# A decoder layer step on one core: page loads as one run, compress weights awaited round by round, a store moved behind the second pages

## The reference

```python
def _compress(rows, w1, b1, w2, b2, pe):          # rows (n, L, 2, 64), L = 1024 (+4), stride 16, window 32
    sub = rows[:, :n_sub * 16].reshape(n, n_sub, 16, 2, 64)
    first = einsum('nspgd,pdh->nsgh', sub, w1[:16])
    second = einsum('nspgd,pdh->nsgh', sub, w1[16:])
    hid = first[:, :-1] + second[:, 1:] + (einsum('pd,pdh->h', pe, w1) + b1)
    return einsum('ncgh,hd->ncgd', gelu(hid), w2) + b2
```

## Time and profile before

| | |
|---|---|
| median of 3 runs | 1866.27 us (1863.54 to 1869.59) |
| the profiled execution's own time | 1865.92 us |
| its span, first to last instruction | 1863.8 us |
| TensorE busy | 1775.2 us, 95% |
| VectorE busy | 938.5 us, 50% |
| ScalarE busy | 544.7 us, 29% |
| mean granted clock of TensorE | 0.977 |
| DMA packets | 98308, of them under 512 B 40637 |
| moved | 145.60 MB |

### The profile page before, as it was taken

How to read it: one execution, slowest core, us unless ns; L and a number is a source line. 1 busy time by engine, 2 the same in 40 slices (tenths; PEclk the granted TensorE clock), 3 DMA queues, 4 the chain that set the end, 5 groups by cost and what they waited for, 6 DMA issues and landing times. The chain is left out here.

```text
span 1863.8 us, 28616 instructions
## 1 busy us (share of the span) xinstructions
PE 1775.2 (95%) x12010; PEld 1625.7 (87%) x12010; DVE 938.5 (50%) x1876; ACT 544.7 (29%) x1098; POOL 249.8 (13%) x110
## 2 busy tenths in 40 slices
PE   8999989589999899999978999999999999999997
PEld 6889978357767769999848999999999999999996
DVE  6422130467787664341533455545545555554547
ACT  7421000168888622210432221111111111111221
POOL 0111200000000000000000023313313322322320
PEclk9999999779999999999989999999999999999998
DMA  5122657621102241110261111101101101101102
GB/s 197 38 72 58 211 140 198 194 92 58 57 24 72 92 155 60 35 57 29 108 248 46 46 51 69 57 12 68 57 12 68 61 8 68 69 2 67 57 17 94
DMA packets 98308, 145.60 MB, mean 78 GB/s; under 512 B 40637, under 2 KB 73597, under 8 KB 96541
## 3 DMA queue, kind: packets, MB, share of 16 engines
q1 hardware_dynamic: 94094, 140.62, 22.7%
q10 hardware_dynamic: 4088, 3.17, 0.6%
HBM read 132.69 MB, written 14.19 MB: 79 GB/s over the span
## 5 line engine op out<-in xcount | busy, mean ns | idle before, releaser
L1963 PE MATMUL ps<-ff_in_high,ff_weights_low 128*128 128x352 f32 x1032 | 335.0, 325 | 0.0
L1963 PE MATMUL ps<-ff_in_high,ff_weights_high 128*128 128x352 f32 x1032 | 332.6, 322 | 0.0
L1963 PE MATMUL ps<-ff_in_low,ff_weights_high 128*128 128x352 f32 x1032 | 330.5, 320 | 0.0
L1963 PEld LDWEIGHTS ps<-ff_in_high,ff_weights_high 128*128 128x128 f32 x1032 | 194.4, 188 | 0.2
L1963 PEld LDWEIGHTS ps<-ff_in_low,ff_weights_high 128*128 128x128 f32 x1032 | 194.0, 188 | 0.2
L1963 PEld LDWEIGHTS ps<-ff_in_high,ff_weights_low 128*128 128x128 f32 x1032 | 193.7, 188 | 0.0
L2195 DVE TENSOR_TENSOR x<-ps,x 128x352 f32<-128x352 f32 x216 | 113.3, 524 | 134.6 <-PE ps L1981 134.6
L1932 POOL TENSOR_TENSOR ff_weights_low<-ff_weights,ff_weights_high 128x1024 fp32r<-128x1024 f32 x44 | 105.7, 2402 | 418.1 <-ACT ff_weights_high L2077 418.1
L1981 PE MATMUL ps<-ff_act_high,ff_down_high 128*128 128x352 f32 (+1 forms) x496 | 158.4, 319 | 0.2
L1981 PE MATMUL ps<-ff_act_high,ff_down_low 128*128 128x352 f32 (+1 forms) x496 | 156.6, 316 | 0.0
L1981 PE MATMUL ps<-ff_act_low,ff_down_high 128*128 128x352 f32 (+1 forms) x496 | 156.6, 316 | 0.0
(11 more groups left out here) (360 smaller groups left out, 3723.4 us busy)
## 6 DMA issues: line engine op xcount, KB each, us to landing
ff_weights<-in_w_up SPq DMA_DIRECT2D x22, 512.0 KB, 4.0
ff_weights<-in_w_gate SPq DMA_DIRECT2D x22, 512.0 KB, 4.3
ff_down<-in_w_down SPq DMA_DIRECT2D x22, 512.0 KB, 3.5
top<-in_mem_kt SPq DMA_DIRECT2D x8, 1024.0 KB, 10.9
top<-in_mem_v SPq DMA_DIRECT2D x8, 1024.0 KB, 13.5
x<-in_xt SPq DMA_DIRECT2D x3, 1408.0 KB, 10.0
x<-in_pool_cmp SPq DMA_DIRECT2D x32, 128.0 KB, 3.1
big<-in_pool_cmp SPq DMA_DIRECT2D x32, 128.0 KB, 2.8
```

The lines of the kernel that those rows point to most:

```text
L1963: last = nc.tensor.matmul(K.bank[3 * s + x][:, 0:b - a], wt[:, s, ws], h[:, k, a:b], start=k + n == 0, stop=k == KD - 1 and n == 2)
```

## The change

It has five parts. `gather` copies a page as one run of 1 KB a partition, so that in SBUF pages follow one another, each with its keys and values (and heads) inside; TensorE's operands of the compress rounds, of `score` and of the value products are rearranged to match. The gains are loaded behind the first quarter of `w_v`, and ScalarE and VectorE wait for them later; ScalarE makes one copy of `eps` ahead of its first wait. TensorE waits for the values' compress weights ahead of the second round; the bias column is made separately for keys and values, each behind its round, with a second buffer for `terms`, and ScalarE's second GELU waits for the second one. The store of `FM[:, 4:8]` moves from the end of mixer_inputs to compress_phase, behind the windows of the first four sequences.

```diff
...
     regs = K.page_regs = K.page_regs or [sp.alloc_register(f"page{b}") for b in range(NPAGE)]
-    slots = K.slots[half]
-    if name == "cmp":
-        slots = slots.rearrange("p v (g t) -> p v g t", g=HKV)
     with sp.Fori(first, first + count) as n:
...
             of = K.pools[name][bass.ds(page, 1)]
-            of = of.rearrange("a p v g t -> (a p) v g t" if name == "cmp" else "a p v t -> (a p) v t")
-            to = slots[:, :, :, bass.ds(n * (NPAGE * PAGE // 2) + b * (PAGE // 2), PAGE // 2)] if name == "cmp" else \
-                slots[:, :, bass.ds(n * (NPAGE * PAGE) + b * PAGE, PAGE)]
+            of = of.rearrange("a p v g t -> (a p) (v g t)" if name == "cmp" else "a p v t -> (a p) (v t)")
+            to = K.slots[half][:, bass.ds(n * (NPAGE * 2 * PAGE) + b * (2 * PAGE), 2 * PAGE)]
             sp.dma_start(to, of).then_inc(K.slots_came[half], 16)
...
-            sp.dma_start(K.gains[:, :, :], I["gains"]).then_inc(const_came, 16)
             for kk in range(4):
...
                 sp.dma_start(wv_landing[kk], I["w_v"][kk]).then_inc(wv_came[kk], 16)
+                if kk == 0:
+                    sp.dma_start(K.gains[:, :, :], I["gains"]).then_inc(const_came, 16)
                 sp.dma_start(K.XT[:, 2 * kk:2 * kk + 2, a:b], I["xt"][:, 2 * kk:2 * kk + 2, a:b]).then_inc(x_came[kk], 16)
...
             sp.dma_start(K.cmp_w1[1], I["w_cmp1"][1]).then_inc(K.cmp_w1_came[1], 16)
-            sp.wait_ge(taken, 3 * CHUNKS)
-            sp.dma_start(O["fm"].rearrange("c p n -> p c n"), K.FM[:, 4:8, :]).then_inc(K.out_sem, 16)
-            K.outs(6)
+            K.outs(5)
             sp.wait_ge(K.gates_sem, 16)
...
-            act.wait_ge(const_came, 16)
+            act.wait_ge(eps_set, 1)
+            nc.scalar.activation(K.stat[:, 0, 0:1], K.eps[:, :], ACT.Copy)
             for kk in range(4):
...
                 nc.scalar.activation(wv[:, 0, 2 * kk:2 * kk + 2, :], wv_landing[kk], ACT.Copy).then_inc(wv_high, 1)
+                if kk == 0:
+                    act.wait_ge(const_came, 16)
                 x_part(0, 2 * kk)
...
-def compress_phase(nc, K, I):
+def compress_phase(nc, K, I, O):
...
     ar = K.big[:, O_HT:BIG]
-    pages = [K.slots[half][:, v].rearrange("p (g t) -> p g t", g=2) for half in range(2) for v in range(2)]
+    pages = [K.slots[half].rearrange("p (b v g q c) -> p v g b q c", v=2, g=2, q=8, c=8)[:, v] for half in range(2) for v in range(2)]
     w1 = K.cmp_w1
...
     pe_w1, summed, vch = S("cmp_pe_product"), S("cmp_pe_sums"), S("cmp_dve")
-    terms = ar[:, 16384:18432].rearrange("p (q h) -> p q h", h=P)
+    terms = [ar[:, o:o + 2048].rearrange("p (q h) -> p q h", h=P) for o in (16384, 8192)]
     c = K.x_tail
...
             sample_windows(sp, K, I, 0)
+            sp.dma_start(O["fm"].rearrange("c p n -> p c n"), K.FM[:, 4:8, :]).then_inc(K.out_sem, 16)
+            K.outs(1)
             sp.wait_ge(first, 2)
...
                 dve.wait_ge(came_w[v], 16)
-                link(nc.vector.tensor_tensor(terms, w1[v], pe_t[v].unsqueeze(2).to_broadcast([P, 16, P]), ALU.mult))
-                link(nc.vector.tensor_reduce(sums[v], terms.rearrange("p q h -> p h q"), AX.X, ALU.add))
+                link(nc.vector.tensor_tensor(terms[v], w1[v], pe_t[v].unsqueeze(2).to_broadcast([P, 16, P]), ALU.mult))
+                link(nc.vector.tensor_reduce(sums[v], terms[v].rearrange("p q h -> p h q"), AX.X, ALU.add))
                 dve.sem_inc(summed, 1)
-            for v in range(2):
                 dve.wait_ge(pe_w1, v + 1)
...
             for n, (v, half) in enumerate(rounds):
-                if n == 0:
-                    act.wait_ge(biased, 2)
+                if n < 2:
+                    act.wait_ge(biased, n + 1)
                 m = 2 * NCMP if half is None else 8 * NCMP
...
             pe.wait_ge(came_w2, 16 * CMP_OPERANDS)
-            def bias():
-                for v in range(2):
-                    pe.wait_ge(summed, v + 1)
-                    nc.tensor.matmul(K.bank[6 + v][:, v:v + 1], sums[v], ones, start=True, stop=True).then_inc(pe_w1, 1)
+            def bias(v):
+                pe.wait_ge(summed, v + 1)
+                nc.tensor.matmul(K.bank[6 + v][:, v:v + 1], sums[v], ones, start=True, stop=True).then_inc(pe_w1, 1)
...
                         for g in range(2):
-                            rhs = src[:, g, :].rearrange("p (b q c) -> p b q c", q=8, c=8)[:, :, q % 8, :]
+                            rhs = src[:, g, :, q % 8, :]
                             at = 1 - q // 8
...
-            for v in range(2):
-                pe.wait_ge(came_w[v], 16)
             for n in range(len(rounds)):
+                if n < 2:
+                    pe.wait_ge(came_w[n], 16)
                 hidden_rows(n)
-                if n == 0:
-                    bias()
+                if n < 2:
+                    bias(n)
                 if n >= 1:
...
             def score(half):
-                KS, VS = K.slots[half][:, 0], K.slots[half][:, 1]
+                KS = K.slots[half].rearrange("p (b v t) -> p b v t", v=2, t=PAGE)[:, :, 0]
                 KW, VW = K.windows[half]
...
                         bank, a, keys = ((2, 64, K.KCS[:, s, :]), (2, 0, K.FM[:, 6, SEQ:T]), (2, 32, K.FM[:, 7, SEQ:T]),
-                                         (0, 0, KS[:, n * 1024:n * 1024 + 512]), (1, 0, KS[:, n * 1024 + 512:n * 1024 + 1024]),
+                                         (0, 0, KS[:, 8 * n:8 * n + 4]), (1, 0, KS[:, 8 * n + 4:8 * n + 8]),
                                          (3, 0, KW[:, n]))[kind]
-                        last = nc.tensor.matmul(K.bank[bank][32 * n:32 * n + 32, a:a + keys.shape[1]], qbd[:, s, :], keys,
+                        last = nc.tensor.matmul(K.bank[bank][32 * n:32 * n + 32, a:a + math.prod(keys.shape[1:])], qbd[:, s, :], keys,
                                                 start=True, stop=True)
...
             for half in range(2):
-                VS, VW = K.slots[half][:, 1], K.windows[half][1]
+                VS, VW = K.slots[half].rearrange("p (b v t) -> p b v t", v=2, t=PAGE)[:, :, 1], K.windows[half][1]
...
                         if i < 8:
-                            v = VS[:, (n * 8 + i) * P:(n * 8 + i + 1) * P]
+                            v = VS[:, n * 8 + i]
                         elif i < 10:
...
-        K.slots = [a.rearrange("p (v n) -> p v n", v=2) for a in (x[:, 0:8192], K.big[:, O_HT:O_HT + 8192])]
+        K.slots = [x[:, 0:8192], K.big[:, O_HT:O_HT + 8192]]
         K.slots_came = [K.sem(f"pages_half{i}") for i in range(2)]
...
         mixer_inputs(nc, K, I, O)
-        compress_phase(nc, K, I)
+        compress_phase(nc, K, I, O)
         sample_attention(nc, K, I)
```

## The result

| | before | after |
|---|---|---|
| median of the runs on one chip | 1866.58 us (1863.54 to 1869.59, 4 runs) | 1846.2 us (1845.3 to 1847.11, 4 runs) |
| ratio, 95% interval | | 0.9894 (0.9879 to 0.9909) |
| span of the profiled execution | 1863.8 us | 1843.6 us |
| mean granted clock | 0.977 | 0.984 |
| DMA packets, of these under 512 B | 98308, 40637 | 65540, 7869 |

The kernel became 20 us faster, five times the 3.9 us that was forecast, and lies outside the range. It went beyond rival three too.

The account below looks back on a forecast made before the run. TensorE's product chain and SyncE's issue chain both reach the compress phase's end, so a gain on TensorE alone stops at SyncE. 1865.92 - 1.5 (start) - 1.8 (SyncE) - 0.2 (landing) = 1862.4 us; range 1857.0 to 1867.5.

Parts of the forecast that it names:

- rival three: Gathers: pages issue faster as one run a partition, 0.16 us off each of 96 issues, giving 1851.8 us; chance 0.07.
- The page's issue: Gathers on SyncE: a page of 128 runs of 1 KB still takes 566 ns to issue, no gain.
- The chain on TensorE: Compress block: without the 6.86 us wait for weights, round 4 comes at 287.5 instead of 294.89, 7.4 us earlier.
- SyncE was to close the block: Compress block's end: SyncE ends at 324.1, behind VectorE's 321.8, so the next gather comes only 1.8 us earlier.
- Start: Kernel's head: early table load and weights ahead of gains bring the first product to 6.1 from 7.82; 1.5 us taken.
- The eight copies: SyncE at the compress block's start: the split's copies take 6.0 us instead of 8.15, middle of 3.7 and 8.15.
- rival one: SyncE is freed too: copies at 0.46 each, 3.7 us in all, no stall from the store; 1859.0 us; chance 0.20.
- rival two: Only the start pays: the copies cost 8.15 us by themselves, TensorE's 7.4 become a page wait; 1864.0 us; chance 0.22.
- The store's own issue: Moved store on SyncE behind the windows: 0.45 us of issue plus 1.05 of stall, 1.5 in the sum.
- Rival four: The moved store chokes SyncE's queue, so its next gather starts 10 us late; 1874.2 us; chance 0.06.
- The clock in a new wait: TensorE waits 3.2 us for pages before round 4; its clock falling there was named as a sign of being wrong.
- The longer stride of the operands: Compress products: operand runs 1 KB apart cost 0; bad end 10%, 5.6 us over four rounds, mostly hidden.

Follow-up runs that it names:

- mark off: Changed kernel with its own shapes and 1 KB runs, the builder told not to prepare the page DMAs' descriptors: 1857.16 us, ratio 0.9955 to the kernel before.
- two-sided kernel: Kernel before with only the pools' DRAM layout changed, so both sides of a page copy keep 128 rows, with the old runs: 1857.54 us, ratio 0.9961.
- store experiment: Changed kernel with the FM store back at the end of mixer_inputs, ahead of the eight copies: 1847.3 us, ratio 0.9901 to the kernel before.
- second experiment: Changed kernel with the page copies and operands of the kernel before, the other three parts kept: 1865.61 us, ratio 1.0006 to the kernel before.

## Why the prediction was wrong, by its own steps

**The page's issue: the step that failed.** "Halving the runs changed nothing, so I take 128 runs at 566 too." The two rows that were equal, 566 and 566, agreed in something else than their cost per run: both forms had a folded source against a destination of 128 rows, and neither was prepared by the builder. So the sum carried a gain of 0 for the issue, and let SyncE close the block, where the runs show 224 ns a page. The runs that took each cause alone: folding away and mark on, with the old pieces, 382; mark off with the new shape, 497; all together, 342. Rival three had the outcome, shorter issues, with a chance of 0.07 and 0.16 us an issue, bounded by the plain issue of 0.41; it is 0.224 us, so 0.41 was the price of other, unlike DMAs and no floor. Its reason, fewer runs, is not what the runs bear out. The gathers shortened by 7.2, 5.6 and 7.0 us, not by 5.

**What followed from it.** The chain on TensorE was right: forecast for round 4 was 287.5 less the start's 1.5, so 286.0, measured 285.88; the 31.1 us from there lead to 317.0, and VectorE's last add ends there:

```profile
316.28 0.68 DVE L735 TENSOR_TENSOR top<-ps,x 63x512 f32<-63x512 f32 x1 [0.84 <-PE ps L803]
```

The forecast discarded this because SyncE was to close the block. SyncE is done at 311.83, so TensorE's gain arrives in full: 9.0 us at the last gather's first page, where I had 1.8 and the start. To that come 7.0 from the last gather, which the forecast held at 0.2, and 4.3 from there to the end of the span (20.2 less 15.9), for which neither forecast nor rival had a term; the forecast's range allowed 2 us for the clock there. The rows place them. Behind the scores 24 products take 2.75 us where they took 4.26, and 16 take 5.39 where they took 6.61; by the prompt's attention the lead is 17.9. In the attention the kernel before shows a granted clock of 0.57, 0.50, 0.50 and 0.73 in the four stretches of 5 us from 385 to 405, the changed kernel 0.50 only in the two from 370 to 380 and 0.99 to 1.00 on either side. The same eight products then start 20.0 apart, before and after:

```profile
358.71 4.26 PE L910 MATMUL ps<-big 128*32 128x512 f32 x24
...
413.47 1.56 PE L1139 MATMUL ps<-top 64*128 64x512 f32 x8 [0.27 <-DVEq L1243]
```

```profile
393.44 1.56 PE L1137 MATMUL ps<-top 64*128 64x512 f32 x8 [0.27 <-DVEq L1241]
```

So most of the 4.3 us, as far as these rows go, is time that TensorE no longer spends at its lower level; why the clock stayed low for less time isn't shown.

**The gains don't add.** Pages alone gave 10.2 us, the other three parts nothing (0.8 slower, within its interval), all together 20. About 10 us exist only in the pair: two chains, TensorE's and SyncE's, reach the block's end together, and each hides the other's gain. I had written so in the first part ("a gain on TensorE alone stops at SyncE") and then the forecast priced only one of the two; rival three priced the pair, 7.4 and 5.0, and fell short by the size of the issue's gain and by the clock.

**Start.** Forecast 1.5 us, with the first product at 6.1. The table load moved as said and the weights landed at 4.17. But I had x's first part issued 0.46 earlier too; the gains now stand ahead of it, and its issue is at 1.64 as before (1.65). ScalarE then waits for x, 1.81 us here. The profiled execution shows no gain at the first product; the compress weights were issued 1.0 earlier although that product was not. The count of TensorE's products in a microsecond shows where they come from, first before, then after, in the windows' view:

```profile
13.00:14.00 1.00, 1.00 (x4) 0.76 (x3) 1.00 (x2) 1.00 (x2) 0.00 (x0) 1.00 1.00 411
14.00:15.00 1.00, 1.00 (x6) 0.81 (x5) 1.00 (x3) 0.86 (x2) 0.00 (x0) 1.00 0.97 391
```

```profile
11.00:12.00 1.00, 1.00 (x5) 0.82 (x4) 1.00 (x2) 1.00 (x2) 0.00 (x0) 1.00 1.00 384
12.00:13.00 1.00, 1.00 (x6) 0.80 (x5) 0.97 (x3) 0.80 (x3) 0.00 (x0) 1.00 1.11 416
```

It reached its quick rate, six products a microsecond for three or four, at about 14 us before and between 11 and 12 after, with the same column of the granted clock, 1.00. By the other kernels this is scatter and no effect of the change: the two-sided kernel, with the old start, reached it between 11 and 12 too, and the kernel with the mark off, with the new one, only at 13. Over all kernels the early table load is worth 0.67 us at the first product, the distance of the means above. At the issue of the values' compress weights, behind the mixer's last product, the four kernels with the old start stand at 248.30, 248.52, 247.42 and 247.96 (mean 248.05), the six with the early table load at 247.27, 247.13, 247.65, 246.10, 246.84 and 247.23 (mean 247.04): 1.0 us, where the sum had 1.5. With the start as it was the median rose by 1.9, not resolved.

**SyncE's other terms.** The eight copies: 6.0 forecast, 5.99 measured, which is luck, since 6.0 was the middle between two ends; rival one's 3.7 and rival two's 8.15 fall. The rows of the copies in the two kernels of the store experiment show why: with the store outstanding their median is 886 ns, without it 597. The store's own issue: 1.5 forecast with its stall, 2.35 measured, and the sel gather behind it still has an issue of 1.29 us. Rival four's choking, 10 us, did not come. With the old pages (the second experiment) the windows' five loads took 5.96 us from 288.30 to 294.26 where I took 3.49 with a gap; with the store's 2.23 and the cmp gather's 30.50 this puts the last gather at 328.95 and not at 324.0 (325.5 less the start's 1.5). So even for pages at 566 the forecast of 1862.4 was too low; the kernel gives 1865.6. Rival two's 1864.0 is nearest to that, but not by its reason: the copies took 5.92 us there, not 8.15. Why the windows' loads cost more there than in the kernel before, 2.77 for four against 5.12, was not settled.

**The clock in a new wait.** For pages at 566 ns the forecast had a wait of 3.2 us in front of round 4 and no price for the clock. In the second experiment TensorE waited 8.02 us: the last compress page was issued at 287.5, but the slowest landing in the view of its compress pages is 6.3 us and not 2.7. It then took 16.00 for the round (granted clock 0.63 from 294 to 299 us), as it did behind 6.86 us in the earlier trace rows. The prediction named this as a sign that it is wrong. In the changed kernel it stood 1.07 us and took 14.05.

**The longer stride of the operands.** 14.05 to 14.08 us for 64 products in every round, as forecast: no cost. The landing: for sel pages a median of 3.4 against 2.7 us, no gain where I had 0.2.

The Trainium skill's rule in "DMA: Bandwidth & Descriptors", section Issuing engines are not separate DMA queues, that initiating a DMA is usually small relative to the DMA itself, fits one page, with 0.566 us of issue and 2.7 us to its landing, but doesn't tell what a row of 32 costs, as the earlier trace rows show. With the same bytes, the same pieces and a landing of 3.1 us, the two-sided kernel is 7.3 us faster, with an issue of 382 ns.

## What to carry to other kernels

Where one engine issues many DMAs in a row, read the duration of one issue by tile and compare it between differently shaped DMAs of the same size; equal durations of two forms say nothing about a third, so try both sides written as the same plain rows before arguing from the count of pieces. When two chains end within a microsecond of each other, price each edit with the other chain at its new length too: a pair of edits can bring 20 us where its halves bring 10 and nothing. A stall taken off one engine, tried by itself, may be a null result that a second edit turns into the larger half.

## What the runs showed of the hardware

- The time in which SyncE issues a page of 128 KB goes with the form of the DMA; within a form, 512 and 256 pieces cost the same: 342 ns (128 rows of 1 KB on both sides, prepared), 382 (128 rows on both sides with two inner dimensions, prepared), 497 (the form of 342, not prepared by the builder), 566 (folded source, not prepared).
- The same store of 2.1 MB takes 0.40 us to issue ahead of the copies and 2.0 to 2.4 behind the windows' 2 MB. Single page issues reach 1.29 us in the changed kernel and 1.96 in the kernel with the store ahead of the copies; why wasn't tested.
- 2.1 MB of store ahead of eight small copies raises their landing from 2.4 to 7.0 us.
- The first part of x is issued at 1.64 or 1.65 us in the five kernels with the new order of loads, and the first product, which waits for it, starts at 6.8 to 7.9 us: a microsecond of scatter at a start that is the same in all five.
- TensorE's products reach their quick rate between 10 and 14 us in the ten kernels, at a granted clock shown as 1.00 throughout.
